# Softmax attention by pairs of heads: values as the stationary operand, probabilities scaled by GpSimd, and the output projection started amid the last turns

## What is computed

```python
def causal_attention_blocks(q, k, v):
    ...
        s = jnp.einsum('bhqd,bhkd->bhqk', q[:, :, lo:hi], k[:, :, :hi]).astype(jnp.float32)
        mask = jnp.arange(hi)[None, :] <= jnp.arange(lo, hi)[:, None]
        p = jax.nn.softmax(jnp.where(mask, s, -jnp.inf), axis=-1).astype(v.dtype)
        outs.append(jnp.einsum('bhqk,bhkd->bhqd', p, v[:, :, :hi]))
...
    o = jnp.concatenate([o_mla.transpose(0, 2, 1, 3).reshape(B, S, MLA_HEADS * MLA_V),
                         o_moba.transpose(0, 2, 1, 3).reshape(B, S, MOBA_W)], axis=-1)
    return o @ w_o
```

## Time and profile before

| what | value |
|---|---|
| median of 3 runs | 859.2 us (859.01 to 859.8) |
| the profiled execution's own time | 859.88 us |
| its span | 858.1 us |
| TensorE busy (matmuls) | 848.4 us, 99% |
| VectorE busy | 603.1 us, 70% |
| ScalarE busy | 440.9 us, 51% |
| GpSimd busy | 116.8 us, 14% |
| DMA | 155.92 MB, mean 182 GB/s |
| chain that ended last | TensorE 94%, VectorE 3% |

### The profile page before, as it was taken

How to read it: one execution, slowest core, us unless ns; L and a number is a source line. 1 busy time by engine, 2 the same in 40 slices (tenths; PEclk the granted TensorE clock), 3 DMA queues, 4 the chain that set the end, 5 groups by cost and what they waited for, 6 DMA issues and landing times.

```text
span 858.1 us, 12970 instructions
## 1 busy us (share of the span) xinstructions
PE 848.4 (99%) x5412; PEld 716.2 (83%) x5412; DVE 603.1 (70%) x742; ACT 440.9 (51%) x575; POOL 116.8 (14%) x74
## 2 busy tenths in 40 slices
PE   8999999999999999999999999999999999999998
PEld 7887888888668887888988899998888888888886
DVE  5694577866557678888798788776876675666653
ACT  5644565667744656753644446352364644444451
POOL 0100001310000014114054344441000000000000
PEclk9999999999999999999999999999999999999999
DMA  9927745545105437226555665657787465555521
GB/s 329 363 94 245 245 148 196 196 148 188 58 1 181 157 99 245 98 84 205 179 177 180 221 198 203 203 188 215 211 300 243 151 224 182 186 190 194 196 99 49
DMA packets 68403, 155.92 MB, mean 182 GB/s; under 512 B 3145, under 2 KB 6954, under 8 KB 68346
## 3 DMA queue, kind: packets, MB, share of 16 engines
q1 hardware_dynamic: 65312, 146.80, 51.0%
q0 software_dynamic: 2224, 7.67, 2.6%
q10 hardware_dynamic: 810, 0.63, 0.4%
HBM read 146.70 MB, written 7.34 MB: 180 GB/s over the span
## 4 chain that ended last, share of the span: by engine, by line
PE 94%; DVE 3%; DMA 1%; ACT 1%; issue 0%; SPq 0%; ACTq 0%; DVEq 0%
PE bank L787 18%; PE bank L788 18%; PE bank L789 18%; PE bank L1156 7%; PE bank L1149 7%; PE bank L1154 4%; PE bank L1152 4%; PE bank L780 3%; PE bank L1346 3%; PE bank L902 2%; DMA ring<-in_a_w_in 1%; PE bank L1270 1%; PE bank L1303 1%; PE bank L890 1%; PE bank L1032 1%; PE bank L944 1%
## 5 line engine op out<-in xcount | busy, mean ns | idle before, releaser
L1871 DVE TENSOR_TENSOR wlo<-ring,whi 128x2048 fp32r<-128x2048 f32 (+1 forms) x103 | 251.8, 2449 | 125.8 <-ACT whi L1464 125.5
L1464 ACT ACTIVATE whi<-ring 128x2048 fp32r<-128x2048 f32 (+1 forms) x104 | 198.4, 1908 | 202.9 <-PE bank L789 134.1
L787 PE MATMUL bank<-whi,hT 128*128 128x512 f32 (+1 forms) x480 | 189.9, 396 | 1.9 <-DVE wlo L2099 1.9
L789 PE MATMUL bank<-whi,hT 128*128 128x512 f32 (+1 forms) x480 | 186.4, 388 | 0.0
L788 PE MATMUL bank<-wlo,hT 128*128 128x512 f32 (+1 forms) x480 | 186.4, 388 | 0.0
L1156 PE MATMUL bank<-hT,wlo 128*128 128x256 f32 x512 | 144.2, 282 | 0.0
L787 PEld LDWEIGHTS bank<-whi,hT 128*128 128x128 f32 x480 | 90.1, 188 | 22.6 <-DVE wlo L2099 3.1
L789 PEld LDWEIGHTS bank<-whi,hT 128*128 128x128 f32 x480 | 90.1, 188 | 18.4
L788 PEld LDWEIGHTS bank<-wlo,hT 128*128 128x128 f32 x480 | 90.2, 188 | 17.8 <-issue 0.7
L1156 PEld LDWEIGHTS bank<-hT,wlo 128*128 128x128 f32 x512 | 97.4, 190 | 0.3
L1149 PE MATMUL bank<-hT,whi 128*128 128x512 f32 x256 | 90.4, 397 | 0.0
(11 more groups left out here) (305 smaller groups left out, 1138.2 us busy)
## 6 DMA issues: line engine op xcount, KB each, us to landing
ring<-in_w_ff SPq DMA_DIRECT2D x64, 1024.0 KB, 5.4
ring<-in_ple_gate_w SPq DMA_DIRECT2D x8, 1024.0 KB, 5.1
ring<-in_w_kv SPq DMA_DIRECT2D x8, 1024.0 KB, 5.0
ring<-in_b_w_in SPq DMA_DIRECT2D x8, 1024.0 KB, 5.0
ring<-in_a_w_in SPq DMA_DIRECT2D x7, 1024.0 KB, 12.8
ring<-in_w_in SPq DMA_DIRECT2D x6, 1024.0 KB, 5.3
ring<-in_w_glu SPq DMA_DIRECT2D x6, 1024.0 KB, 8.3
ring<-in_a_w_out SPq DMA_DIRECT2D x4, 1024.0 KB, 5.9
```

The costliest lines, as they stand in the source:

```text
L787: pe.matmul(bank_cols, high[:, at[0], at[1]], w_high, start=first, stop=False)
L789: return pe.matmul(bank_cols, low[:, at[0], at[1]], w_high, start=False, stop=last)
L1464: act.activation(whi[at], raw_rows(g), ACT.Copy).then_inc(high_made, 1)
L1871: dve.tensor_tensor(wlo[at], raw_rows(g), whi[at], ALU.subtract).then_inc(low_made, 1)
```

## The change

- The loop goes over pairs c (0 to 7): scores, maxima (one VectorE operation for two heads), copies of the turned probabilities (one for two heads). `AHEAD` = 3 now counts pairs.
- The values are stationary, in the form of `stick_values`; their product comes out turned, in the bank of `("T", "o2", m)`, and the turns of `h` go. `soft_out` goes.
- VectorE makes one reciprocal a head, GpSimd scales that head's probabilities in place by two products (128x128, 128x256) before TensorE turns them. `probs` has six buffers, `probsT` four, and lies in `h`.
- The turns of the MoBA queries and keys come at pairs 2 to 5. VectorE's quarter splits come two at a time, in its rounds 5 and 7.
- The last three pairs' turns and values have pieces of w_o's first block between them (`out_piece`, six products each).
- `constant_products` goes, and GpSimd's table 0 waits for the first bank of f1's step 0.

```diff
-MOBA_TURNS = {4: ("qmoba", 0), 5: ("qmoba", 1), 6: ("kmoba", 0), 7: ("kmoba", 1)}
+MOBA_TURNS = {2: ("qmoba", 0), 3: ("kmoba", 0), 4: ("qmoba", 1), 5: ("kmoba", 1)}
-KEEP = (37, 12, 6)
+KEEP = (12, 6)
...
+    for c in range(MH + AHEAD + 1):
+        if c in MOBA_TURNS:
+            u.add(("T",) + MOBA_TURNS[c], "a", bank=7 if c > 2 else 4)
+        if c < MH:
+            for odd in range(2):
+                u.add(("scores", 2 * c + odd), "a", bank=2 * (c % 2) + odd)
+        if c < 2:
+            u.add(("T", "qmla", 2 + c), "a", bank=4 + 2 * c)
+            u.add(("T", "kmla", 2 + c), "v", bank=5 + 2 * c)
+        if c > AHEAD and (c - AHEAD) % 2 == 0:
+            m = (c - AHEAD) // 2 - 1
+            u.add(("T", "o2", m), "av", bank=6 + m % 2)
+        if AHEAD <= c < MH + AHEAD:
+            for odd in range(2):
+                u.add(("probsT", 2 * (c - AHEAD) + odd), "v", bank=4 + odd)
...
+            def probs_turned(c):
+
+                for n in (2 * c, 2 * c + 1):
+                    b = begin(("probsT", n))
+                    pe.wait_ge(probs_scaled, 2 * n + 2)
+                    for k in range(3):
+                        last = pe.transpose(b[:, k * P:(k + 1) * P], probs[:, n % 6, k * P:(k + 1) * P], ident)
                     last.then_inc(pe_done, 1)
...
+                for o, vh, a in sides:
+                    pe.matmul(o, vh[:, 0, :], a[:, 0:S], start=True, stop=False, skip_group_check=True)
+                for o, vh, a in sides:
+                    last = pe.matmul(o[:, P:S], vh[:, 1, :], a[:, S:384], start=False, stop=True, skip_group_check=True)
+                if c % 2:
+                    last.then_inc(pe_done, 1)
...
+                if c < 2:
+                    soft_turns(2 + c)
+                if c > AHEAD:
+                    soft_values(c - AHEAD - 1)
+                if c >= AHEAD:
+                    probs_turned(c - AHEAD)
...
+                for k in ks:
+                    if t == 0 and k % 2 == 0:
+                        emptied(("T", "o2", k // 2))
+                    last = three(out_sums[t][:, :], (hT_hi, hT_lo), (k, slice(t * P, t * P + P)), w_high[:, k % 4, :],
+                                 w_low[:, k % 4, :], k == 0, k == KC - 1)
...
+            out_piece(0, (0, 1))
+            soft_values(MH - 4)
+            probs_turned(MH - 3)
+            out_piece(1, (0, 1))
+            soft_values(MH - 3)
+            probs_turned(MH - 2)
+            out_piece(0, (2, 3))
+            soft_values(MH - 2)
+            probs_turned(MH - 1)
+            out_piece(1, (2, 3))
+            soft_values(MH - 1)
+            for ks in ((4, 5), (6, 7)):
+                for t in range(NT):
+                    out_piece(t, ks)
+            product("w_o", 1, ("w_o", 1), between=lambda: turn(("ffn", 0), x, units=(0, 1), ready=x_has("w_o")))
...
-            constant_products(("ug", 0), KEEP[0], 32)
...
+                for i in (2 * c, 2 * c + 1):
+                    b = filled(("scores", i))
+                    act.wait_ge(max_ready, c + 1)
+                    if i >= 6:
+                        act.wait_ge(pe_done, done(("probsT", i - 6)))
...
+            for c in range(MH + AHEAD):
+                if c < MH:
+                    maxima(c)
+                if 0 < c <= MH:
+                    reciprocals(2 * c - 1)
+                if c < 2:
+                    turned_out("kmla", [(turned_qk["mla"][1], "kn_mla", True)], units=(2 + c,), width=MQK)
+                if c >= AHEAD:
+                    filled(("probsT", 2 * (c - AHEAD) + 1))
+                    at = 2 * ((c - AHEAD) % 2)
+                    dve.tensor_copy(probsT[:, at:at + 2, :], bank_pair("probsT", c - AHEAD)).then_inc(dve_emptied, 2)
+                if c < MH:
+                    reciprocals(2 * c)
+                if c == 1:
                     row_scale("kmoba", 4 + 4)
+                if c in (6, 8, 10):
+                    turned_low("o2", None, (c // 2 - 3,))
+                if c in (5, 7):
+                    refill_piece("wv", 0, c - 5)
+                    refill_piece("wv", 0, c - 4)
+            turned_low("o2", None, (3,))
...
-            pool.wait_ge(pe_done, done(("soft_out", 3)))
+            for i in range(2 * MH):
+                n, head = divmod(i, MH)
+                pool.wait_ge(rden_ready, i + 1)
+                for t, cols in enumerate((slice(0, P), slice(P, 384))):
+                    a = probs[:, i % 6, cols]
+                    pool.tensor_tensor(a, a, rden[:, n, head, t:t + 1].broadcast_to([P, cols.stop - cols.start]),
+                                       ALU.mult).then_inc(probs_scaled, 1)
+            pool.wait_ge(pe_done, done(("T", "o2", 3)))
...
-                if f:
-                    pool.wait_ge(pe_done, done((("f1", 0, f), 0, 0)))
+                pool.wait_ge(pe_done, done((("f1", 0, f), 0, 0)))
```

More of the change, by code:

```diff
@@ L253, in plan @@
     soft_plan(u)
-    turned_in_two(u, "o2")
-    rolled(u, "w_o", ("ffn", 0), "v")
+    u.turn += 6
+    for nb in range(2):
+        if nb:
+            turned_in_two(u, ("ffn", 0), (0, 1))
+        for t in range(NT):
+            u.add(("w_o", nb, t), "v", **({} if nb else {"bank": t}))
     mlp_plan(u, 0)
@@ L294, in soft_plan @@
     u.add(("wv", 0, 1), "a", bank=3)
[L295 to L311, removed]
+    for c in range(MH + AHEAD + 1):
[13 more added lines that the diff above has]
+                u.add(("probsT", 2 * (c - AHEAD) + odd), "v", bank=4 + odd)
+    for m in range(3):
+        u.freed_in_order([("probsT", 4 * m + 4 + k) for k in range(4)] + [("T", "o2", m)])
 def hidden_bank(layer, i):
@@ L1069, in moba_scores @@
-            def moba_scores(i):
-                pair = [begin(("scores", i + odd)) for odd in range(2)]
+                emptied(("T", "qmla", c))
+                emptied(("T", "kmla", c))
+                for i in (2 * c, 2 * c + 1):
+                    b = begin(("scores", i))
+                    pe.matmul(b[:, 0:P], tq[0:MQK, i, 0:P], tk[0:MQK, i, 0:P], start=True, stop=False, skip_group_check=True)
+                    pe.matmul(b[:, P:P + S], tq[0:MQK, i, P:S], tk[0:MQK, i, :], start=False, stop=False,
+                              skip_group_check=True)
+                    score_masks(i, b)
@@ L1079, in moba_scores @@
                 for b, r in zip(pair, rows):
-                    pe.matmul(b[:, P:P + S], tq[r, c, P:S], tk[r, c, :], start=False, stop=False, skip_group_check=True)
+                    pe.matmul(b[:, P:P + S], tq[r, k, P:S], tk[r, k, :], start=False, stop=False, skip_group_check=True)
                 for odd, b in enumerate(pair):
[L1082 to L1090, removed]
@@ L1106, in _ @@
[L1106 to L1118, removed]
+                    score_masks(2 * c + odd, b)
@@ L1119, in _ @@
+            for c in range(MH):
+                if c in MOBA_TURNS:
+                    name, k = MOBA_TURNS[c]
                     turn(name, qb if name == "qmoba" else kb, units=(k,),
                          ready=lambda k: pe.wait_ge(heads_normed, 5 if name == "qmoba" else 8))
[L1121 to L1124, removed]
+                if c < MH // 2:
+                    mla_scores(c)
+                else:
+                    moba_scores(c)
+                if c < 2:
[4 more added lines that the diff above has]
+                    probs_turned(c - AHEAD)
@@ L1366, in _ @@
             emptied(("inject", 3))
-            for _ in range(KEEP[2]):
+            for _ in range(KEEP[1]):
                 pe.matmul(bank(("inject", 2))[:, 0:P], allneg[:, :], allneg[:, :], start=True, stop=True,
@@ L2407, in _, with maxima, reciprocals @@
-            turned_low("o2", None)
+            def maxima(c):
+                n, head = divmod(2 * c, MH)
+                filled(("scores", 2 * c + 1))
+                both = bank_pair("scores", c)
+                dve.tensor_reduce(nmax[:, n, head:head + 2, 0], both[:, :, 0:P], AX_X, ALU.max, negate=True)
+                dve.tensor_reduce(nmax[:, n, head:head + 2, 1], both[:, :, P:384], AX_X, ALU.max, negate=True)\
+                    .then_inc(max_ready, 1)
+            def reciprocals(i):
+                n, head = divmod(i, MH)
+                emptied(("scores", i))
+                dve.reciprocal(rden[:, n, head, :], den[:, n, head, :]).then_inc(rden_ready, 1)
```

120 lines of the change are left out of this document (48 added, 72 removed).

## The result

The changed kernel takes **863.12 us** (median of 6 runs, 862.99 to 863.34) against 859.21 (6 runs, 858.93 to 859.8): ratio 1.0046, 95% interval 1.0033 to 1.0059. It is slower by 3.9 us. The forecast was 856.7 us with a range to 861.0, and slower had 0.16.

What follows compares the result with a forecast made beforehand. TensorE was taken to bound the kernel, in the loop with VectorE not far behind. Loop -5.6, constant products -0.4 and later table +3.5 sum to -2.5 us, from 859.2 to 856.7 us; range 852.6 to 861.0.

Steps and rivals of the forecast that it cites:

- Values stationary, no o2 turns, GpSimd's scaling: Softmax loop: values at 0.80 us a pair save 3.5 us, dropped o2 turns 2.2; GpSimd scales at 0.96 us a head.
- The loop, -5.6 us: Loop through w_o's first half ends at 389.5 instead of 395.0, with bounds of -3.5 and -6.2 us.
- The walk: Engines' new loop orders laid side by side, each operation starting when engine and inputs are ready; found 3.1 us of waits.
- The constant products, -0.4: Dropping 37 products at 601.73 lets the first turn start some 0.4 us sooner; between 0 and -1.2 us.
- GpSimd's first table later, +3.5: Table behind the first f1 bank delays VectorE's injection operations, so TensorE waits 2.9 us, then 1.3 for low parts.
- as if the two engines took turns for whole operations: VectorE and GpSimd, both reading two SBUF operands, alternate by whole operations; basis of the later table's 2.9 us wait.
- rival 4: Clock falls to 1.2 GHz behind the 3 us wait, f2's first half taking 5.5 us more: 862.2 us; chance 0.07.
- Rival 1: Later table is hidden, since VectorE gives way to nobody or has more slack: 853.2 us; chance 0.24.
- Moving it away gains nothing there: Table's old place behind the loop slows two VectorE splits, but TensorE waits for neither, so moving it gains nothing.

Runs made afterwards that it cites:

- e11: e6 with the four first pieces of w_o all put behind the last values instead of amid the last turns; 859.31 us.
- e3: Kernel before, with only the 37 constant products taken out; 859.16 us, ratio 1.0012.
- e2: Kernel before, with only GpSimd's first table made to wait for the first bank of the first f1 block; 868.04 us.
- e6: Changed kernel, with GpSimd's first table behind the last bank of w_o's second block; 854.45 us.
- e10: Changed kernel, table back right behind the loop, each of the table's half products waiting for the product before it; 854.24 us.
- e12: Kernel before, with only GpSimd's first table moved behind the last bank of w_o's second block; 859.28 us.
- e1: Changed kernel, with GpSimd's first table back in its early place right behind the loop; 856.26 us.
- e5: Changed kernel, late table kept, each half product of GpSimd's tables waiting for the product before it; 859.76 us.
- e8: Changed kernel, with each of GpSimd's 32 scaling products issued twice; 872.03 us.
- e9: e6 with the 37 constant products put back ahead of the first turns of chunks; 857.68 us.
- e7: Changed kernel, with 29 filler products on TensorE ahead of its wait at the first injection turn; 861.70 us.

## Why the prediction was wrong

- **Values stationary, no o2 turns, GpSimd's scaling: right.** 0.80 us a pair; 0.97 us a head against 0.96.
- **The loop, -5.6 us: measured -4.5**, inside its bounds. The sum had 5.7 us of removed instructions, and 3.1 us of waits and gaps in place of 2.9. Added up in the same way, the trace of after leaves 4.0 us (40.78 less some 36.8 of instructions): 1.3 are three waits that the profile names (0.30, 0.66, 0.37), 0.7 are the pieces, each of which costs 0.18 us more than its six products (1.55 from 376.21 to 377.76), and the rest are small gaps between instructions. And e11 shows that what was removed would have been given back as waits for VectorE's copy (5.0 us of them there, 0.4 in after), had w_o's pieces not filled them. The walk had the pieces as the reason why the last turns are not waited for; it put no price on them, and they carry all of the gain. That the term came near its number is in part luck.
- **The constant products, -0.4: 0.2 in the medians** of the old kernel (859.16 against 859.36 on the same chip), which is not clear of the spread. In after, the first turn of chunks does come 0.4 us sooner, as the term says; in e3's trace it does not. The 1.1 us that after gets back behind the MLP come mostly from the stop of 1.07 us, which that execution does not have.
- **GpSimd's first table later, +3.5: measured +8.9 (e2) and +8.7 (after less e6). This is the step that failed**, in two terms. The wait was sized at 2.9 us at the turn, and 1.3 behind it for the low parts, which did not come. At the turn it was 6.73, because of the sentence "as if the two engines took turns for whole operations": in turns, VectorE stands behind one GpSimd operation each time. In the trace it stood behind three. The row that I read for it groups two splits. Taken singly, VectorE and GpSimd in the kernel before:

```profile
386.65 5.06 DVE L1871 TENSOR_TENSOR wlo<-ring,whi 128x2048 fp32r<-128x2048 f32 x1 [0.79 <-ACT whi L1464]
```

```profile
385.13 2.18 POOL L2597 TENSOR_TENSOR work<-pa,cs 128x1152 f32<-128x1152 f32 x1
387.24 1.19 POOL L2600 TENSOR_TENSOR aux<-pb,cs 128x576 f32<-128x576 f32 x1
388.37 1.19 POOL L2600 TENSOR_TENSOR aux<-pb,cs 128x576 f32<-128x576 f32 x1
389.63 4.61 POOL L2602 TENSOR_TENSOR work<-work,aux 128x1152 f32<-128x1152 f32 x1
```

The split waits 2.77 us, until about 389.4, where GpSimd's third operation ends, and gets in only where GpSimd itself has a wait (ahead of L2602). Walked with that, the wait for the second table in the injection would have been for three products, some 4.5 us and not the 2.2 of its first alone. In the trace the injection's third operation had that wait, and its fourth then stood behind the second table's last product as well (2.3 us more): 9.3 us lost in the injection against 4.8 in the walk. The second term is the clock: rival 4 had it, at 0.07 and in place of the forecast. It is no rival of the stall but its consequence, worth 2.1 us and not 5.5, since the clock was back at full at about 437.5, some 7 us after its fall.
- **Rival 1** (the later table hidden, 853.2 us) is nearly what e6 and e10 come to in other ways, at 854.45 and 854.24; in the place the change gives it, it was wrong.
- **"Moving it away gains nothing there"** was right for the old kernel (e12) and wrong for the new one (1.8 us, e1): I asked it of the old timeline, in which TensorE came 5 us later.

The Trainium skill (page SBUF — State Buffer, section SBUF: two separate sides) holds that the pair of ports is an exclusive lock, which whichever operation starts first has for its whole instruction; of VectorE's operations those with two SBUF inputs (and those in a 2-port mode) contend for it with GpSimd, and the others do not. The traces agree on the lock and on who contends: 4.47 us for three whole operations, and 0.68 us as ever for VectorE's addition with a PSUM bank at 413.29, with GpSimd's product in flight from 411.68 to 415.39. On who comes first the profile's starts do not fit it for L2106, which starts 0.20 us ahead of GpSimd's product and is the one that waits. I had the lock from there; that the two engines alternate was an assumption of mine.

## What to carry to other kernels

When two engines share a resource by whole instructions, take a clash apart one instruction at a time before sizing it, and price the worst case against the other engine's whole run of instructions up to its next wait; a wait for the instruction just issued is a cheap way to let the other engine in. Price a stall with what the clock does behind it, not as a rival to it. And when a change makes a loop shorter, ask anew of everything behind it whether its old cover still reaches; here a place between the two tried kept all of the gain, 854.45 us against 859.3 before and 863.1 after.

## What the runs showed that was not expected

- VectorE can stand behind three queued GpSimd operations (5.69 us for an operation of 1.22) and, elsewhere, between two of them; a wait in GpSimd's queue brought it down to 3.46.
- The granted clock fell in waits and in stretches behind them: behind 6.73 us of wait in after and e2, 3.3 in e5 (0.50 at 430 to 431), and 1.78 in e8, where shorter waits had gone before; it did not behind 1.36 in e1.
- Executions of one and the same kernel differed by whether their mean clock was lower: 5 to 6 us apart in e3 (three of 12), 3 to 4 in e9 (six of 12), and in single executions of e5 (864.47 and 867.29 us, clock 0.994 and 0.990), e7 (867.76, 0.994) and e11 (866.32, 0.990). The kernel before (29 executions in the last group) and after (6, all at 0.994 to 0.996 by their stall) had no such split.
